# Two batches of turned page keys and the scaled sample heads placed ahead of the first output group, their key pages ahead of value pages

## Time and profile before

| | |
|---|---|
| median of three runs | 1653.86 us (1653.48 to 1657.52) |
| the profiled execution | 1651.47 us |
| its span, first to last instruction | 1649.5 us |
| PE busy | 1502.7 us (91%) |
| DVE busy | 619.6 us (38%) |
| ACT busy | 284.3 us (17%) |
| chain that ended last | PE 64%, DMA 25%, DVE 6%, ACT 4% of the span |
| HBM | 305 GB/s over the span |

### The profile page before, as it was taken

How to read it: one execution, slowest core, us unless ns; L and a number is a source line. 1 busy time by engine, 2 the same in 40 slices (tenths; PEclk the granted TensorE clock), 3 DMA queues, 4 the chain that set the end, 5 groups by cost and what they waited for, 6 DMA issues and landing times.

```text
span 1649.5 us, 20694 instructions
## 1 busy us (share of the span) xinstructions
PE 1502.7 (91%) x8388; PEld 650.7 (39%) x8388; DVE 619.6 (38%) x1142; ACT 284.3 (17%) x646; POOL 48.4 (3%) x62
## 2 busy tenths in 40 slices
PE   7999999898999989799999989889889889889996
PEld 3544554554444655533333333233323323323322
DVE  2056885353230532633333233233223322423325
ACT  3114335451210321200000000000010000000002
POOL 3000000001010000000000000000000000000000
PEclk9999999999999999889999999999999999999999
DMA  7311220459371278479999999999999999999994
GB/s 239 137 57 52 83 99 14 166 198 335 128 259 52 77 274 336 141 303 428 426 428 428 428 429 427 427 429 428 428 428 428 429 428 427 429 428 427 430 427 192
DMA packets 70077, 500.06 MB, mean 303 GB/s; under 512 B 6960, under 2 KB 7520, under 8 KB 45568
## 3 DMA queue, kind: packets, MB, share of 16 engines
q1 hardware_dynamic: 59136, 468.47, 69.0%
q0 software_dynamic: 7760, 23.92, 4.1%
q10 hardware_dynamic: 3120, 6.82, 1.1%
HBM read 491.97 MB, written 11.14 MB: 305 GB/s over the span
## 4 chain that ended last, share of the span: by engine, by line
PE 64%; DMA 25%; DVE 6%; ACT 4%; issue 1%; SPq 0%; ACTq 0%; DVEq 0%; POOLq 0%
PE psum L2684 17%; DMA r_h<-w 11%; PE psum L2123 10%; DMA ring<-w 9%; PE psum L2109 8%; PE psum L2699 7%; PE psum L2747 6%; PE psum L2218 3%; DMA r_mix<-w 2%; PE psum L2658 1%; PE psum L2094 1%; ACT r_c L1264 1%; DVE ring L1471 1%; PE psum L2469 1%; PE psum L2486 1%
## 5 line engine op out<-in xcount | busy, mean ns | idle before, releaser
L2684 PE MATMUL psum<-ring,r_c 128*64 128x512 f32 x1504 | 340.5, 599 | 20.2 <-DMA ring<-w 19.0
L2747 PE MATMUL psum<-ring,r_c 128*64 128x512 f32 x768 | 172.5, 597 | 32.6 <-ACT r_c L1277 21.4
L2684 PEld LDWEIGHTS psum<-ring,r_c 128*64 128x64 f32 x1504 | 104.6, 137 | 243.5 <-issue 215.2
L1988 DVE TENSOR_TENSOR r_x<-r_x,psum 128x1024 f32<-128x1024 f32 x64 | 78.0, 1221 | 264.4 <-PE psum L2699 264.3
L2109 PE MATMUL psum<-r_h,ring 128*128 128x512 f32 x320 | 140.9, 600 | 1.9 <-ACT r_h L905 1.9
L1272 ACT ACTIVATE r_c<-psum 128x512 f32<-128x512 f32 x32 | 19.1, 598 | 597.1 <-PE psum L2684 597.1
L2699 PE MATMUL psum<-r_c,early 64*128 64x512 f32 x496 | 119.4, 608 | 0.0
L2006 DVE TENSOR_SCALAR r_c<-r_c 128x512 f32<-128x512 f32 x32 | 13.5, 422 | 277.8 <-ACT r_c L1272 277.8
L2123 PE MATMUL psum<-ring,r_h 128*128 128x512 f32 x256 | 111.5, 594 | 1.1 <-DMA ring<-w_in 1.1
L2008 DVE RECIPROCAL r_c<-r_c 128x512 f32<-128x512 f32 x32 | 107.3, 3353 | 1.1
L2747 PEld LDWEIGHTS psum<-ring,r_c 128*64 128x64 f32 x768 | 52.3, 137 | 136.2 <-issue 90.3
(11 more groups left out here) (380 smaller groups left out, 1452.6 us busy)
## 6 DMA issues: line engine op xcount, KB each, us to landing
ring<-w SPq DMA_DIRECT2D x141, 2048.0 KB, 33.1
r_mix<-w SPq DMA_DIRECT2D x24, 2048.0 KB, 32.1
r_h<-w SPq DMA_DIRECT2D x24, 2048.0 KB, 31.6
ring<-w_in SPq DMA_DIRECT2D x6, 2048.0 KB, 10.2
ring<-cache_mem_v SPq DMA_DIRECT2D x8, 1024.0 KB, 10.1
ring<-cache_mem_k POOLq DMA_DIRECT2D x8, 1024.0 KB, 7.1
ring<-cache_moba_v SPq DMA_DIRECT2D x24, 256.0 KB, 6.6
ring<-w_xk SPq DMA_DIRECT2D x2, 2048.0 KB, 7.7
```

Of the source, the lines that this page charges most:

```text
L1988: return dve.tensor_tensor(x, x, psum_t[:, bank:bank + 2, :].rearrange("p a n -> p (a n)"), ALU.add)
L2684: ins = pe.matmul(psum[2 + 2 * u + m][CAP * half:CAP * (half + 1), :], xT[:, k, CAP * u:CAP * (u + 1)], (first_row(2 + m, kk) if first els ...
L2747: ins = pe.matmul(psum[7][CAP * half:CAP * (half + 1), :], heT[u][:, k % 4, CAP * (k // 4):CAP * (k // 4 + 1)], moe_place(place)[:, kk, 51 ...
```

## The change

In all five streams and in the job list the same two moves: the turned keys of batches 2 and 3, and with them `scores(0)` on PE and `sample_heads_normed` on DVE, go ahead of the output groups (0,0) and (0,1); and SP asks for the key pages of batches 3 and 4 ahead of the value pages of batches 3 and 2. The heads are still turned on PE behind group (0,1). The number and the shapes of the instructions are the same.

```diff
--- before.py
+++ after.py
@@ -198,11 +198,11 @@
     add("A", "o", NT)
     all_of("A", "hgT", range(NT))
     all_of("V", "Us", range(8))
+    keys_turned("KT", 2)
+    keys_turned("KT", 3)
     add("V", "x1", 0, 0)
-    keys_turned("KT", 2)
     add("V", "x1", 0, 1)
     add("A", "hgT", NT)
-    keys_turned("KT", 3)
     add("V", "Sn", 0)
     add("V", "x1", 0, 2)
     keys_turned("KT", 4)
@@ -683,14 +683,14 @@
             J.wait_filled(sp, "OT", 3)
             sp.wait_ge(out_mv, 32)
             key_pages(2)
+            J.wait_filled(sp, "KT", 0, 3)
+            key_pages(3)
+            J.wait_filled(sp, "KT", 1, 3)
+            key_pages(4)
             sp.wait_ge(s0_in, 16)
             value_pages(3)
             sp.wait_ge(out_memk[1], 16)
             value_pages(2)
-            J.wait_filled(sp, "KT", 0, 3)
-            key_pages(3)
-            J.wait_filled(sp, "KT", 1, 3)
-            key_pages(4)
             J.wait_filled(sp, "hgT", NT - 1)
             value_pages(0, 1)
             for b in (5, 6, 7):
@@ -1133,8 +1133,8 @@
             for i in range(NT):
                 turn_heads(i)
             keys_turned(2)
+            keys_turned(3)
             turn_heads(NT)
-            keys_turned(3)
             sample_exps(0)
             keys_turned(4)
             sample_probs(0)
@@ -1678,12 +1678,12 @@
             gate_applied(NT)
             for n in range(8):
                 sample_states(n)
+            keys_turned(2)
+            keys_turned(3)
+            sample_heads_normed()
             dve.wait_ge(xr_in[0], 16)
             add_rows("x1", 0, 0)
-            keys_turned(2)
             add_rows("x1", 0, 1)
-            sample_heads_normed()
-            keys_turned(3)
             sample_probs(0)
             dve.wait_ge(xr_in[1], 32)
             add_rows("x1", 0, 2)
@@ -2399,15 +2399,15 @@
             for i in range(NT):
                 turn_heads(i)
             sample_states(range(8))
+            pe.wait_ge(qx_done, 1)
+            scores(0)
+            keys_turned(2)
+            keys_turned(3)
             J.wait_emptied(pe, "OT", NT - 1)
             J.wait_emptied(pe, "hgT", NT - 1)
             rows_summed(0, 0)
-            keys_turned(2)
-            pe.wait_ge(qx_done, 1)
-            scores(0)
             rows_summed(0, 1)
             turn_heads(NT)
-            keys_turned(3)
             scores(2)
             new_scores(0)
             rows_summed(0, 2)
```

## The result

The changed kernel takes 1646.18 us (median of six runs, 1641.29 to 1651.29) against 1654.80 for the kernel before in the same runs (1652.62 to 1660.09): ratio 0.9944, 95% interval 0.9925 to 0.9963, so 6.1 to 12.4 us less (the ratio is taken over all runs; that of the two medians is 0.9948). Predicted were 1646.1 us and a gain of 7.8. The profiled execution took 1646.42 us, its span 1644.6. The times of one kernel go with its mean granted clock: in the runs taken together with after_again (see the experiments), ten of 23 executions of the kernel before had a clock of 0.980 to 0.984 and took 1656.1 to 1661.7 us, the other 13 had 0.986 or 0.987 and a median of 1652.25, and all six of the changed kernel had 0.987 or more and a median of 1644.90, so at a like clock the gain there is 7.35 us and not the 8.22 of the medians.

What follows compares the result with a forecast made beforehand. PE's 6.97 us stall behind DVE's wait for x delays the expert-weight stream; 8.0 us saved less 0.2 for hand-overs gives 7.8, taken off the 1653.86 median: 1646.1 us, range 1643.5 to 1650.3.

Steps and rivals of the forecast that it cites:

- The stall is DVE's order, not the reload itself: PE's 6.97 us stall: copies of keys 2 and scaled heads stand behind DVE's 15.37 us wait for x.
- The sum on PE: From 370.99, output group (0,2) begins at 394.4, not 402.38: 8.0 us, less 0.2 for hand-overs, keeps 7.8.
- the pace of the states: DVE frees one sample-state bank each 1.05 us, holding turned keys 3 until 378.0, a 1.3 us cost on PE.
- Keys 3 need the place of value pages 3: In SP's queue, that place lands key pages 3 by 373.2; PE wants them at 375.0, so no cost.
- the upper bound: If pages of batch 3 land behind both value batches, at 379.4, PE stands 4.4 us at keys 3.
- The states, priced at nothing: Earlier key pages beside the sample states' landing near 363.36: bounds zero to 5.4 us, zero taken.
- The rows of x have until 398.6: With two adds and DVE's softmax following, the rows may land as late as 398.6 without loss.
- 3.1 MB beside the rows, priced at nothing: Keys 6 and the second half of output weights move beside the rows of x from 378.0; no cost taken.
- backlog first: Rival: q0 waits for q1's older work, second rows 8 us later at 405.5; gain 5.4, 1648.5 us; chance 0.10.
- Slower: Rival: keys 6 and output weights starve the rows of x; 1665.3 us at a one-quarter share; chance 0.06.
- Swallowed by the stream: Rival: the expert weights end when they did despite the earlier start, 1653.9 us; chance 0.07.
- The clock at 1.00 throughout: Sign in the trace after: PE's granted clock stays at 1.00, not 0.52 as after the old stall.

Runs made afterwards that it cites:

- after_again: The changed kernel run once more, unaltered, as yardstick on the same chip; ratio 0.9938 to the kernel before.
- before_no_states: The kernel before without writing the samples' new states to memory, so POOL loads the rows of x earlier; ratio 0.9944 to the kernel before.
- reload_late: The changed kernel with POOL held back from loading the rows of x until PE has filled output group (0,1); ratio 0.9978 to the kernel before.
- pages_only: The kernel before with only SP's changed order, key pages 3 and 4 ahead of value pages 3 and 2; ratio 0.9996 to the kernel before.
- compute_only: The changed kernel with SP's old order, value pages 3 and 2 ahead of key pages 3 and 4; ratio 0.9974 to the kernel before.
- keys2_only: The changed kernel with turned keys 3 moved back behind the two output groups, keys 2 and heads still ahead; ratio 0.9980 to the kernel before.
- after_no_states: The changed kernel without writing the samples' new states to memory, so the rows of x load earlier; ratio 0.9938 to the kernel before.
- scores4_early: The changed kernel with the scores of batches 4 and 5 also moved ahead of output group (0,3); ratio 0.9925 to the kernel before.

## Why the prediction was right, point by point

- *The stall is DVE's order, not the reload itself.* Shown: before_no_states shortens it by an earlier reload (6.97 to 1.56 us), the change removes it by the order, and the two don't add.
- *The sum on PE, 8.0 us, kept as 7.8.* Measured 8.27. The two output groups started where the sum had them, at 378.0: 379.61 less the 1.59 us by which the first state update came later here. So the pace of the states was right (1.09 us of it show as the three waits). What differs is small: the groups took 13.74 us and not 13.9, the terms behind 378.0 add up to 394.3 and not 394.4, and of the 0.2 us taken off for hand-overs nothing shows.
- *Keys 3 need the place of value pages 3.* Right in both directions: no wait for a page on PE in the changed kernel, 4.74 us without the changed place, where the upper bound said 4.4.
- *The states, priced at nothing.* Right: PE's wait at that place was 1.46 us before and is 1.02 in the changed kernel (1.25 in after_again).
- *The rows of x have until 398.6.* Right: in the changed profile PE takes the softmax at 404.42, 4.5 us of adds and softmax lie before it, so the rows had until 399.9 and came at 394.0; reload_late pays only what goes beyond.
- *3.1 MB beside the rows, priced at nothing.* Right in the result, in part by luck: the prediction let SP ask for the 3.1 MB at 378.0 and gave SP's issuing no time, and SP came to them only at 389.44 and 394.93. So the change itself hardly tests the rival "backlog first" (whose 405.5 should read 405.0 by its own terms). reload_late does: there SP asked for the second half of `w_out` at 389.5, POOL for the rows of x only at 393.53, and the first rows landed after 8.8 us, `w_out` 20.7 us after its issue, at 410.2. So the older backlog on q1 does not go first, and the rival falls. But the rows moved nothing until 397 there, much as the states from 374 to 378 before the change and after it. Why a transfer on q0 begins so late is unexplained.
- *Slower* needed q0's share under one third; from 378 to 397 it had 55% (4.12 of 7.53 MB).
- *Swallowed by the stream* falls: from the first expert product (L2684 in the chain of waits, before and then after) to the end of the span it is 944.7 us before and 945.1 after, so an earlier start ends earlier.

```profile
704.76 16.33 PE psum L2684 x64
...
699.54 16.46 PE psum L2684 x64
```

- *The clock at 1.00 throughout* was wrong. It held where the prediction worked it out, and failed at 428 us, at an idle time that the change doesn't touch. The local gain of 8.27 us is 6.7 by the end of this stretch. The prediction had given a lower clock behind the stretch no price; it cost 1.6 us. That the timed gain (8.6 us by the medians) came out near the forecast is therefore partly luck: the other 1.9 us lie outside this stretch, where no trace shows a gain, and the times can't tell 6.7 from 8.

What stays open is why that clock fell. The same 2.30 us of idle time stand in the profiles of before, pages_only, compute_only, keys2_only and before_no_states without that effect, and in those of after, after_again, after_no_states and reload_late with it. Whether the clock had fallen earlier in the stretch doesn't decide it: in before_no_states it had not (1.00 from 394 to 404) and it held, in reload_late it had (at 406) and it fell again. No run moved the idle time alone. Open, too, is what `scores(0)` and the scaled heads bring by themselves: no run moved them without keys 2.

## What to carry to other kernels

When an engine that works in order waits for a transfer, look at what stands behind the wait and who needs it; work that doesn't need the transfer goes ahead of it, and its own inputs have to be asked for earlier in the same edit, or the wait only changes its name (without that, 6 of the 8 us were lost here). A wait that ends off the critical path may stay long: DVE's is still 12 us. And price a short stall of PE with the clock behind it, which in reload_late made 2.4 us cost 4.7. When transfers are put ahead of others, give the issuing engine its time as well: SP took 12.47 us to issue twelve of them.

## What the runs showed of the hardware that was not expected

Idle time of PE as short as 2.3 and 2.4 us can be followed by the lower level of the clock (granted 0.54 from 428 to 430, behind 2.30 us, in after; 0.64 from 406 to 410, around 2.41 us, and 0.63 from 430 to 434, around 2.30 us, in reload_late). It need not be: in five other profiles 2.30 us at the same place were followed by 1.00. Behind 1.38 us in scores4_early it stayed at 1.00.

A transfer that was queued on q0 behind a busy q1 moved next to nothing for some 4 us and then more than half of all bytes: the write of the states in both kernels (issued at 373.21 before, 0.03 MB until 378, then 58% of the bytes until 397; at 374.79 after, nothing until 378), and the rows of x in reload_late (issued at 393.53, nothing until 397, then two thirds of the bytes from 398 to 406).

SP's issues of 256 KB each took 0.47 us apiece for the four key pages of batch 2 (1.88 us) at 360.46 in after, and 1.04 to 1.36 us apiece from 371.58 to 394.88, where value pages 2, 0 and 1, keys 5 and keys 6 followed without a pause. No run shows why.
